# Gate and up products of an expert step in 512 columns instead of 256, with the weight split writing both chunks mixed

## The chip, the cores and the metric

The kernel runs on one core of one Trainium2 chip. The metric is the device time of one execution in microseconds (us), the median of several runs. TensorE is called PE here (its weight loads PEld), VectorE DVE, ScalarE ACT, GpSimd POOL, and SyncE, which issues the weight transfers, SP.

## The reference, cut to what matters

The program computes two model blocks over 256 tokens of width 1024. The last part of the second block is a mixture of eight experts, and it is the part that the change touches:

```python
N_EXPERTS = 8
TOP_K = 2
D_FF_EXPERT = 3584

def swiglu_2(x, w_gate, w_up, w_down):
    return (jax.nn.silu(x @ w_gate) * (x @ w_up)) @ w_down

def moe_swiglu(x, w_router, w_gate, w_up, w_down):
    ...
    for e in range(N_EXPERTS):
        y = y + combine[:, e:e + 1] * swiglu_2(xt, w_gate[e], w_up[e], w_down[e])
    return y.reshape(B, S, D)
```

All inputs are float32. Each expert has 3 x 1024 x 3584 weights, 44 MB.

## The kernel before, in words

The tokens that chose an expert are gathered by a product with a 0/1 matrix into `xe`, at most 128 of them, so that one pass of an expert is a product of 128 rows. A pass is made for each of the 8 experts (and more, if an expert has more than 128 tokens; in the profiled execution there are 8 passes). The first pass is written out, the others are a loop on the engines.

The hidden width of 3584 is walked in 14 steps of 256 (`MOE_PER`). The weights of a step are three chunks of 1 MB, 128 partitions x 2048 float32 each: a **gate** chunk (8 blocks of 128 rows x 256 columns, laid one behind the other), an **up** chunk of the same form, and a **down** chunk (2 blocks of 128 rows x 1024 columns). `MOE_ORDER` sets their order, which all engines follow: gate 0, up 0, gate 1, up 1, then gate s, up s, down s-2 for each step, and the last two downs at the end; 42 chunks in a pass.

A chunk goes through four engines:

- **SP** loads it into one of the 7 slots of `ring` (L510 to L515). It waits on `w_split`, the count of the chunks that are split, until the chunk 7 places before it has been split, and then issues the transfer.
- **ACT** copies it from the ring to `w_h`, rounded to the matmul type (`high_part`, L1237 to L1241). `w_h` and its partner `w_l` have 3 places (`SPLITS`), so the copy of chunk n+3 waits on `w_used`, which the first matmul of chunk n+1 raises. Between the copies ACT makes `silu` of the gate (L1452) and moves the transposed products out of PSUM (L1457).
- **DVE** takes the rest, `w_l` = ring - `w_h` (`low_part`, L1964 to L1968), and raises `w_split`. Between these it multiplies silu(gate) by up (L2064), and makes the rest of the transposed products (L2069).
- **PE** waits on `w_split` and multiplies with both parts. In `half_product` (L1043 to L1054) the stationary operand is a block of the tokens, `xe_h` or `xe_l` (128 x 128), and the moving operand is a block of 256 weight columns of `w_h` or `w_l`. Gate goes to columns 0 to 255 of PSUM bank s % 2, up to columns 256 to 511 of the same bank. For each of 8 row blocks k there are three products:

```python
o = 0 if part == "gate" else 256
out = psum[:, s % 2, o:o + 256]
for k in range(KD):
    first = nc.tensor.matmul(out, xe_h[:, k, :], wh[:, k, :], start=(k == 0), stop=False)
    ...
    nc.tensor.matmul(out, xe_h[:, k, :], wl[:, k, :], start=False, stop=False)
    last = nc.tensor.matmul(out, xe_l[:, k, :], wh[:, k, :], start=False, stop=(k == KD - 1))
```

That is 24 matmuls of 256 columns for a gate chunk and 24 for an up chunk. Both are done before `u_full` is raised, and only then does ACT take the silu. `expert_down` (L1064 to L1079) makes 12 matmuls of 512 columns for a down chunk, in turn into banks 4 and 5, and each matmul loads its own stationary operand. Two transposes (L1060) stand between a step's down and the next gate. A pass also has a gather (L1015), four pairs of matmuls that scatter the expert before it (L1031, L1032) and two more transposes.

Of the kernel before, what the change touches and what calls it, by code (L numbers as in the profile page):

```python
# [35 lines left out]
KD = D // P  # L36
SLOTS = 7
# [4 lines left out]
ALU = mybir.AluOpType  # L42
ACT = mybir.ActivationFunctionType
F32 = mybir.dt.float32
# [11 lines left out]
MOE_E = 8  # L56
MOE_PER = 3584 // 256
MOE_CHUNKS = 3 * MOE_PER
# [3 lines left out]
SPLITS = 3  # L62
# [44 lines left out]

MOE_ORDER = moe_order()
MOE_N = {c: n for n, c in enumerate(MOE_ORDER)}
LAST = MOE_PER - 1  # L110

SCATTER_AT = (3, 6)
# [112 lines left out]
CHUNKS = plan_chunks()  # L225
# [7 lines left out]
MOE_C0 = CHUNK_AT[("k8", "moe_gate", 0)]  # L233
# [4 lines left out]
def build(nc, a, out):  # L238
    with ExitStack() as ctx:
# [7 lines left out]
        ring = sb("ring", [P, SLOTS, CHUNK_F])  # L247
# [28 lines left out]
        psum = ctx.enter_context(nc.psum_tensor("psum", [P, BANKS, BF], F32))  # L276
# [34 lines left out]
        w_l = sb("w_l", [P, SPLITS, CHUNK_F], F32R)  # L311
# [74 lines left out]
        slot_full = [sem(f"slot_full{i}") for i in range(SLOTS)]  # L386
# [45 lines left out]
        w_high = sem("w_high")  # L432
        w_split = sem("w_split")
# [38 lines left out]
        def evacuated(eng, u):  # L472

            n = UNIT_AT[u]
            eng.wait_ge(bank_free[n % BANKS], n // BANKS + 1)

        def halves(ap):
            return ap.rearrange("p (b c) -> p b c", b=2)

# [3 lines left out]
        n = 0  # L483
# [14 lines left out]
        @block.sync  # L498
        def _(sp):

            sp.dma_start(h[:, :, :], a["x"].rearrange("a (b p) d -> p (a b) d", p=P)).then_inc(loads["x"], 16)
            for j in range(SLOTS):
                sp.dma_start(ring[:, j, :], a["stream"][j, :, :]).then_inc(slot_full[j], 16)
            with sp.Fori(1, MOE_C0 // SLOTS + 1) as r:
                for j in range(SLOTS):

                    sp.wait_ge(chunk_used, r * SLOTS - SLOTS + j + 1)
                    sp.dma_start(ring[:, j, :], a["stream"][bass.ds(r * SLOTS + j, 1), :, :]
                                 .rearrange("a p f -> (a p) f")).then_inc(slot_full[j], 16)
            with sp.Fori(MOE_C0 // SLOTS + 1, len(CHUNKS) // SLOTS) as r:  # L510
                for j in range(SLOTS):

                    sp.wait_ge(w_split, r * SLOTS + (j + 1 - SLOTS - MOE_C0))
                    sp.dma_start(ring[:, j, :], a["stream"][bass.ds(r * SLOTS + j, 1), :, :]
                                 .rearrange("a p f -> (a p) f")).then_inc(slot_full[j], 16)  # L515

            sp.wait_ge(table_ready, 1)
            n_over = sp.value_load(table[0:1, 1:2], min_val=0, max_val=OVER)
            with sp.If(n_over > 0):
                with sp.Fori(0, n_over) as p:  # L520
                    e = sp.value_load(table[0:1, bass.ds(p + 2, 1)], min_val=0, max_val=MOE_E - 1)
                    with sp.Fori(0, MOE_CHUNKS // SLOTS) as r:
                        for j in range(SLOTS):
                            sp.wait_ge(w_split, p * MOE_CHUNKS + r * SLOTS + (len(CHUNKS) - MOE_C0 - SLOTS + j + 1))
                            sp.dma_start(ring[:, j, :], a["stream"][bass.ds(e * MOE_CHUNKS + r * SLOTS + (MOE_C0 + j), 1), :, :]
                                         .rearrange("a p f -> (a p) f")).then_inc(slot_full[j], 16)

            for j in range(AHEAD):
                sp.wait_ge(w_split, n_over * MOE_CHUNKS + (len(CHUNKS) - MOE_C0 - SLOTS + j + 1))
                sp.dma_start(ring[:, j, :], a["stream"][MOE_C0 + j, :, :]).then_inc(slot_full[j], 16)  # L530


# [33 lines left out]
        def _(pe):  # L566
# [237 lines left out]
            for u in range(8):  # L804
                open_unit(pe, ("t_b", u))
                for j in range(4):
                    n = 4 * (u % 4) + j
                    last = nc.tensor.transpose(bank(("t_b", u))[:, j * P:(j + 1) * P],
                                               b_wide_f[u // 4][:, n * P:(n + 1) * P], ident[:, :])
# [5 lines left out]
            for u0 in range(0, BLK // 2, 4):  # L815
# [46 lines left out]
            for u in range(4):  # L862
                open_unit(pe, ("sgu", u))
                for j in range(2):
                    hd = 2 * u + j
                    for b in range(TB):
                        o = bank(("sgu", u))[:, j * TOK + b * P:j * TOK + (b + 1) * P]
# [169 lines left out]
            def split_pair(p, part, s, k):  # L1037

                n = MOE_N[(part, s)]
                pe.wait_ge(w_split, p * MOE_CHUNKS + (n + 1))  # L1040
                return [w[:, n % SPLITS, :].rearrange("p (k c) -> p k c", k=k) for w in (w_h, w_l)]

            def half_product(p, part, s):  # L1043
                wh, wl = split_pair(p, part, s, KD)
                o = 0 if part == "gate" else 256
                out = psum[:, s % 2, o:o + 256]
                for k in range(KD):
                    first = nc.tensor.matmul(out, xe_h[:, k, :], wh[:, k, :], start=(k == 0), stop=False)  # L1048
                    if k == 0:
                        first.then_inc(w_used, 1)  # L1050
                    nc.tensor.matmul(out, xe_h[:, k, :], wl[:, k, :], start=False, stop=False)  # L1051
                    last = nc.tensor.matmul(out, xe_l[:, k, :], wh[:, k, :], start=False, stop=(k == KD - 1))  # L1052
                if part == "up":
                    last.then_inc(u_full, 1)  # L1054

            def transpose_h(p, s):
# [24 lines left out]
            def one_expert(p, first):  # L1081

                pe.wait_ge(xe_split, p + 1)
                for s in range(MOE_PER):

                    pe.wait_ge(hT_ready, p * MOE_PER + (f0 + s - 1))
                    half_product(p, "gate", s)
                    half_product(p, "up", s)
                    if s in SCATTER_AT and not first:
                        b = SCATTER_AT.index(s)  # L1090
                        if b == 0:
                            pe.wait_ge(oe_split, p)
                            pe.wait_ge(pickT_ready, p)
                        else:

                            pe.wait_ge(y_added, p * 4 + 2)
                        scatter(p, b, (6, 7))
                    if s == GATHER_AT:

                        pe.wait_ge(pick_ready, p + 2)  # L1100
                        pe.wait_ge(y_added, p * 4 + 4)
                        gather(1)
                    if s == LAST:
                        transpose_h(p, s - 1)
                    if s >= 2:
                        if s == 2 and not first:

                            pe.wait_ge(oe_split, p)
                        expert_down(p, s - 2)
                    if 1 <= s < LAST:  # L1110
                        if s == PICK_AT + 1:

                            pe.wait_ge(pickT_ready, p + 1)
                        transpose_h(p, s - 1)
                    if s == PICK_AT:
                        transpose_pick()
                transpose_h(p, LAST)
                expert_down(p, LAST - 1)
                expert_down(p, LAST)
# [18 lines left out]
        def _(act):  # L1138
# [97 lines left out]

            def high_part(p, n):  # L1237

                act.wait_ge(slot_full[n % SLOTS], p * (16 * MOE_CHUNKS // SLOTS)
                            + 16 * (MOE_C0 // SLOTS + n // SLOTS + 1))  # L1240
                nc.scalar.activation(w_h[:, n % SPLITS, :], ring[:, n % SLOTS, :], ACT.Copy).then_inc(w_high, 1)  # L1241

            parts = [0]

# [63 lines left out]
            for u in range(8):  # L1308
                take_unit(act, ("t_b", u))
                n = 4 * (u % 4)  # L1310
# [186 lines left out]
        def _(dve):  # L1497
# [466 lines left out]
            def low_part(p, n):  # L1964

                dve.wait_ge(w_high, p * MOE_CHUNKS + (n + 1))
                V.tensor_tensor(w_l[:, n % SPLITS, :], ring[:, n % SLOTS, :], w_h[:, n % SPLITS, :].bitcast(F32),  # L1967
                                ALU.subtract).then_inc(w_split, 1)  # L1968


            V.tensor_copy(h_h[:, :, :], h[:, :, :]).then_inc(h_high, 1)
# [264 lines left out]
```

## Time and profile before

| | |
|---|---|
| median of 3 runs | 2394.29 us (2392.45 to 2394.78) |
| profiled execution, its own time | 2396.11 us |
| its span, first to last instruction | 2394.3 us |
| PE busy | 2210.5 us, 92% |
| PEld busy | 2043.9 us, 85% |
| DVE busy | 1563.7 us, 65% |
| ACT busy | 1190.5 us, 50% |
| mean granted clock of PE | 0.957 |
| HBM read | 539.05 MB |

The busy times are unions over the span, so that two overlapping instructions of an engine count once. The busy time of PE includes the modelled end of each matmul; what a matmul costs in a stream is read from the starts of two of them, not from its duration. The eight passes take the stretch from 1323 us to the end.

### The profile page before, as it was taken

How to read it: one execution, taken by the hardware profiler on the slowest of the kernel's cores; microseconds unless marked ns; L12 is line 12 of the kernel's file. 1: busy time of each engine (PE TensorE's matmuls, PEld its weight loads, DVE VectorE, ACT ScalarE, POOL GpSimd, SP SyncE). 2: the span in 40 equal slices, each digit the busy share in tenths (PEclk: the TensorE clock that was granted, in tenths of full speed). 3: DMA queues.
4: the chain of work that ended last, by engine and by line, in shares of the span. 5: the costliest groups of instructions: out<-in, count | busy, mean ns of one | idle time of the engine just before them, and what ended most of it. 6: DMA issues, size and time to landing. Idle time of an engine off the chain costs nothing.

```text
span 2394.3 us, 38794 instructions
## 1 busy us (share of the span) xinstructions
PE 2210.5 (92%) x15310; PEld 2043.9 (85%) x15310; DVE 1563.7 (65%) x1739; ACT 1190.5 (50%) x1206; POOL 9.8 (0%) x22
## 2 busy tenths in 40 slices
PE   7999987799889879989986999999999999999997
PEld 6888787799888779989876999989898998989896
DVE  6774144444555454454645789878787888888787
ACT  2300023334336533433642667767676766667674
POOL 0000000000000000000000000000000000000000
PEclk9999898899989989999997999999999999999998
DMA  7243241355543245554323799989898898989894
GB/s 285 105 152 112 71 157 71 115 184 191 196 176 124 99 137 188 187 199 177 115 97 123 275 358 337 355 310 348 307 351 320 341 339 326 357 311 356 309 348 154
DMA packets 76345, 542.45 MB, mean 227 GB/s; under 512 B 9121, under 2 KB 9265, under 8 KB 11810
## 3 DMA queue, kind: packets, MB, share of 16 engines
q1 hardware_dynamic: 72128, 524.32, 59.2%
q0 software_dynamic: 2080, 10.40, 1.2%
q10 hardware_dynamic: 1986, 5.41, 0.6%
q8 instruction: 132, 2.16, 0.4%
q14 instruction: 19, 0.16, 0.0%
HBM read 539.05 MB, written 1.05 MB: 226 GB/s over the span
## 4 chain that ended last, share of the span: by engine, by line
PE 86%; DVE 6%; ACT 4%; issue 3%; ACTq 0%; DVEq 0%
PE psum L750 11%; PE psum L1071 10%; PE psum L1048 9%; PE psum L1051 9%; PE psum L1052 9%; PE psum L595 6%; PE psum L656 6%; PE psum L642 6%; PE psum L762 5%; PE psum L608 3%; PE psum L621 2%; PE psum L1015 1%; DVE w_l L1967 1%; PE psum L1060 1%; PE psum L585 1%
## 5 line engine op out<-in xcount | busy, mean ns | idle before, releaser
L1967 DVE TENSOR_TENSOR w_l<-ring,w_h 128x2048 fp32r<-128x2048 f32 x338 | 773.7, 2291 | 177.6 <-ACT w_h L1241 176.5
L1241 ACT ACTIVATE w_h<-ring 128x2048 fp32r<-128x2048 f32 x338 | 647.0, 1914 | 166.4 <-PE psum L1048 122.4
L1048 PE MATMUL psum<-w_h,xe_h 128*128 128x256 f32 x1792 | 520.1, 290 | 23.0 <-issue 20.6
L1051 PE MATMUL psum<-w_l,xe_h 128*128 128x256 f32 x1792 | 511.5, 285 | 0.0
L1052 PE MATMUL psum<-w_h,xe_l 128*128 128x256 f32 x1792 | 511.4, 285 | 0.0
L1048 PEld LDWEIGHTS psum<-w_h,xe_h 128*128 128x128 f32 x1792 | 347.6, 194 | 26.0 <-issue 23.1
L1051 PEld LDWEIGHTS psum<-w_l,xe_h 128*128 128x128 f32 x1792 | 347.9, 194 | 0.0
L1052 PEld LDWEIGHTS psum<-w_h,xe_l 128*128 128x128 f32 x1792 | 347.5, 194 | 0.0
L1650 DVE TENSOR_TENSOR wf_l<-ring,wf_h 128x2048 fp32r<-128x2048 f32 x66 | 151.3, 2292 | 168.2 <-ACT wf_h L1235 168.2
L1624 DVE TENSOR_TENSOR wp_l<-ring,wp_h 128x2048 fp32r<-128x2048 f32 x54 | 123.7, 2292 | 168.5 <-ACT wp_h L1253 168.5
L750 PE MATMUL psum<-xf_h,wf_h 128*128 128x256 f32 x704 | 201.4, 286 | 4.5 <-DVE xf_l L1642 2.4
L750 PE MATMUL psum<-xf_l,wf_h 128*128 128x256 f32 x704 | 201.3, 286 | 0.0
L750 PE MATMUL psum<-xf_h,wf_l 128*128 128x256 f32 x704 | 201.2, 286 | 0.0
L1235 ACT ACTIVATE wf_h<-ring 128x2048 fp32r<-128x2048 f32 x66 | 125.9, 1910 | 125.4 <-PE psum L762 65.8
L1253 ACT ACTIVATE wp_h<-ring 128x2048 fp32r<-128x2048 f32 x54 | 103.0, 1910 | 157.5 <-PE psum L656 92.7
L750 PEld LDWEIGHTS psum<-xf_h,wf_h 128*128 128x128 f32 x704 | 137.1, 195 | 6.0 <-DVE xf_l L1642 2.8
L1071 PE MATMUL psum<-w_h,eT_h 128*128 128x512 f32 x448 | 141.2, 396 | 0.0
L1071 PE MATMUL psum<-w_h,eT_l 128*128 128x512 f32 x448 | 138.9, 391 | 0.0
L1071 PE MATMUL psum<-w_l,eT_h 128*128 128x512 f32 x448 | 138.8, 391 | 0.0
L750 PEld LDWEIGHTS psum<-xf_l,wf_h 128*128 128x128 f32 x704 | 137.0, 195 | 0.7
L750 PEld LDWEIGHTS psum<-xf_h,wf_l 128*128 128x128 f32 x704 | 137.0, 195 | 0.0
L656 PE MATMUL psum<-wp_h,xf_h 128*128 128x256 f32 x416 | 120.7, 290 | 16.0 <-DVE xf_l L1629 8.7
(340 smaller groups left out, 3720.7 us busy)
## 6 DMA issues: line engine op xcount, KB each, us to landing
ring<-in_stream SPq DMA_DIRECT2D x499, 1024.0 KB, 4.9
big<-in_bc POOLq DMA_DIRECT2D x11, 512.0 KB, 5.0
big<-in_na_bias POOLq DMA_DIRECT2D x2, 2048.0 KB, 8.0
big<-in_mem ACTq DMA_DIRECT2D x1, 1024.0 KB, 8.5
h<-in_x SPq DMA_DIRECT2D x1, 1024.0 KB, 7.5
r_k<-in_sgu_ln ACTq DMA_DIRECT2D x1, 1024.0 KB, 22.3
big<-in_s_c ACTq DMA_DIRECT2D x1, 1024.0 KB, 30.0
out_dram<-ysum ACTq DMA_DIRECT2D x1, 1024.0 KB, 4.0
```

The source lines that it names most:

```text
L595: last = nc.tensor.matmul(bank(unit)[:, j * TOK:(j + 1) * TOK], w[:, k, j * P:(j + 1) * P], act_T[:, k, :], start=(k == 0), stop=(k == KD ...
L642: last = nc.tensor.matmul(bank(unit)[:, j * TOK:(j + 1) * TOK], w[:, k, j * P:(j + 1) * P], x[:, k, :], start=(k == i == 0), stop=(k == KD ...
L656: last = nc.tensor.matmul(bank(unit)[:, b * 256:(b + 1) * 256], x[:, k, b * P:(b + 1) * P], w[:, k, :], start=(k == i == 0), stop=(k == KD ...
L750: last = nc.tensor.matmul(psum[:, b, j * TOK:(j + 1) * TOK], w[:, k, j * P:(j + 1) * P], x[:, k, :], start=(k == i == 0), stop=(k == KD - ...
L1048: first = nc.tensor.matmul(out, xe_h[:, k, :], wh[:, k, :], start=(k == 0), stop=False)
L1051: nc.tensor.matmul(out, xe_h[:, k, :], wl[:, k, :], start=False, stop=False)
L1052: last = nc.tensor.matmul(out, xe_l[:, k, :], wh[:, k, :], start=False, stop=(k == KD - 1))
L1071: last = nc.tensor.matmul(psum[:, 4 + c, :], x[:, s % 2, k, :], w[:, k, c * 512:(c + 1) * 512], start=(s == 0 and k == n == 0), stop=(s == ...
L1235: nc.scalar.activation(wf_h[:, n % SPLITS, :], ring[:, at % SLOTS, :], ACT.Copy).then_inc(wf_high, 1)
L1241: nc.scalar.activation(w_h[:, n % SPLITS, :], ring[:, n % SLOTS, :], ACT.Copy).then_inc(w_high, 1)
L1650: V.tensor_tensor(wf_l[:, n % SPLITS, :], ring[:, at % SLOTS, :], wf_h[:, n % SPLITS, :].bitcast(F32), ALU.subtract).then_inc(wf_split, 1)
L1967: V.tensor_tensor(w_l[:, n % SPLITS, :], ring[:, n % SLOTS, :], w_h[:, n % SPLITS, :].bitcast(F32), ALU.subtract).then_inc(w_split, 1)
```

## The change

The gate and up products of a step become one product of 512 columns, made in two halves over the rows. Each half takes 4 of the 8 row blocks k and makes three matmuls of 512 columns for each, 12 in all, which fill the whole PSUM bank: gate in its left 256 columns, up in the right ones.

For that, row block k of gate and row block k of up must lie side by side in `w_h` and `w_l`. The chunks in memory and the transfers are the same as before. The split does the mixing: the part called "gate" now takes blocks 0 to 3 of the gate chunk **and** blocks 0 to 3 of the up chunk, the part called "up" takes blocks 4 to 7 of both. It reads the two neighbouring slots of the ring (slots 6 and 0 with a negative step) in runs of 256 elements, and still handles 2048 elements a partition. So the copy of a "gate" part waits for the transfers of two chunks, and neither slot of the pair is free before the "up" part is split: `MOE_FREED` says so to SP, whose loop now runs over passes and names each chunk of a pass. The down chunks are split and used as before.

```diff
+MOE_FREED = [n + 2 if part == "gate" else n + 1 for n, (part, s) in enumerate(MOE_ORDER)]
...
+        def moe_parts(n, high, low):
+            part, s = MOE_ORDER[n % MOE_CHUNKS]
+            to = n % SPLITS
+            if part == "down":
+                return ring[:, n % SLOTS, :], high[:, to, :], low[:, to, :]
+            half = part == "up"
+            at = (n - half) % SLOTS
+            both = ring[:, at:at + 2, :] if at + 1 < SLOTS else ring[:, ::-at, :]
+            src = both[:, :, half * 1024:(half + 1) * 1024].rearrange("p a (k c) -> p a k c", k=4)
+            return (src,) + tuple(w[:, to, :].rearrange("p (k a c) -> p a k c", k=4, a=2) for w in (high, low))
...
-                    sp.wait_ge(w_split, r * SLOTS + (j + 1 - SLOTS - MOE_C0))
+                sp.wait_ge(w_split, p * MOE_CHUNKS + MOE_FREED[n])
...
-            def half_product(p, part, s):
-                wh, wl = split_pair(p, part, s, KD)
-                o = 0 if part == "gate" else 256
-                out = psum[:, s % 2, o:o + 256]
-                for k in range(KD):
-                    first = nc.tensor.matmul(out, xe_h[:, k, :], wh[:, k, :], start=(k == 0), stop=False)
...
+            def half_product(p, half, s):
+                wh, wl = split_pair(p, ("gate", "up")[half], s, 4)
+                out = psum[:, s % 2, :]
+                for i in range(4):
+                    k = 4 * half + i
+                    first = nc.tensor.matmul(out, xe_h[:, k, :], wh[:, i, :], start=(k == 0), stop=False)
...
+                    nc.tensor.matmul(out, xe_h[:, k, :], wl[:, i, :], start=False, stop=False)
+                    last = nc.tensor.matmul(out, xe_l[:, k, :], wh[:, i, :], start=False, stop=(k == KD - 1))
...
             def high_part(p, n):
...
-                act.wait_ge(slot_full[n % SLOTS], p * (16 * MOE_CHUNKS // SLOTS)
-                            + 16 * (MOE_C0 // SLOTS + n // SLOTS + 1))
-                nc.scalar.activation(w_h[:, n % SPLITS, :], ring[:, n % SLOTS, :], ACT.Copy).then_inc(w_high, 1)
+                gate = MOE_ORDER[n % MOE_CHUNKS][0] == "gate"
+                for c in ((n, n + 1) if gate else (n,)):
+                    act.wait_ge(slot_full[c % SLOTS], p * (16 * MOE_CHUNKS // SLOTS)
+                                + 16 * (MOE_C0 // SLOTS + c // SLOTS + 1))
+                src, high, _ = moe_parts(n, w_h, w_l)
+                nc.scalar.activation(high, src, ACT.Copy).then_inc(w_high, 1)
...
             def low_part(p, n):
...
-                V.tensor_tensor(w_l[:, n % SPLITS, :], ring[:, n % SLOTS, :], w_h[:, n % SPLITS, :].bitcast(F32),
-                                ALU.subtract).then_inc(w_split, 1)
+                src, high, low = moe_parts(n, w_h, w_l)
+                V.tensor_tensor(low, src, high.bitcast(F32), ALU.subtract).then_inc(w_split, 1)
```

PE, the seam between the first and the second half of step 0 of the first pass, before (L1048, L1051 and L1052 are the three products of a row block):

```order
L1048 MATMUL psum<-w_h,xe_h 128x256
L1051 MATMUL psum<-w_l,xe_h 128x256
L1052 MATMUL psum<-w_h,xe_l 128x256
L1048 MATMUL psum<-w_h,xe_h 128x256 [waits w_split]
L1051 MATMUL psum<-w_l,xe_h 128x256
L1052 MATMUL psum<-w_h,xe_l 128x256
```

and the same engine from the start of the first pass now, where the three products are L1070, L1073 and L1074:

```order
L1070 MATMUL psum<-w_h,xe_h 128x512 [waits w_split,hT_ready,xe_split]
L1073 MATMUL psum<-w_l,xe_h 128x512
L1074 MATMUL psum<-w_h,xe_l 128x512
L1070 MATMUL psum<-w_h,xe_h 128x512
L1073 MATMUL psum<-w_l,xe_h 128x512
L1074 MATMUL psum<-w_h,xe_l 128x512
```

The order of the three products is the same, each has twice the columns, and there are half as many: the 24 rows of a part became 12.

ACT, one step in the middle of a pass, before (L1241 is the copy to `w_h`, L1452 the silu, L1457 the move of the transposes):

```order
L1241 ACTIVATE w_h<-ring 128x2048 [waits slot_full5,w_used]
L1451 REGISTER_ALU
L1452 ACTIVATE e_silu<-psum 128x256 [waits up_full]
L1480 REGISTER_ALU
L1241 ACTIVATE w_h<-ring 128x2048 [waits slot_full6,w_used]
L1456 REGISTER_ALU
L1457 ACTIVATE eT_h<-psum 128x256 [waits hT_full]
L1480 REGISTER_ALU
L1239 REGISTER_ALU [waits w_used]
L1241 ACTIVATE w_h<-ring 128x2048 [waits slot_full0]
```

and the same step now (L1266, L1477, L1482):

```order
L1266 ACTIVATE w_h<-ring 128x2x4x256 [waits slot_full6,slot_full5,w_used]
L1476 REGISTER_ALU
L1477 ACTIVATE e_silu<-psum 128x256 [waits up_full]
L1505 REGISTER_ALU
L1266 ACTIVATE w_h<-ring 128x2x4x256 [waits slot_full6,w_used]
L1481 REGISTER_ALU
L1482 ACTIVATE eT_h<-psum 128x256 [waits hT_full]
L1505 REGISTER_ALU
L1263 REGISTER_ALU [waits w_used]
L1266 ACTIVATE w_h<-ring 128x2048 [waits slot_full0]
```

No instruction of ACT moved; the copies of gate and up have a pattern of 2 slots x 4 blocks x 256, and the gate copy waits for two slots.

## Rows read from the trace of the kernel before

**Rows 1.** Busy time by stretch; columns: PE, PEld, DVE, ACT, POOL, clock, DMA share, GB/s

```profile
10.00:20.00 10.00, 3.65 (x16) 3.28 (x16) 7.60 (x22) 4.88 (x11) 0.00 (x0) 1.00 1.03 418
1323.00:2394.30 1071.30, 1034.06 (x7280) 967.97 (x7280) 890.51 (x636) 727.10 (x587) 0.00 (x0) 0.98 0.86 324
...
1433.31:1561.12 127.81, 127.81 (x913) 119.77 (x912) 110.10 (x78) 90.56 (x73) 0.00 (x0) 1.00 0.93 346
1561.12:1694.25 133.13, 129.42 (x913) 121.26 (x912) 110.29 (x78) 90.64 (x73) 0.00 (x0) 0.99 0.88 332
...
1486.87:1495.58 8.71, 8.71 (x64) 8.17 (x63) 7.89 (x6) 6.41 (x5) 0.00 (x0) 1.00 0.98 357
```

**Rows 2.** Waits, 1340 to 2390 us: who waited for whom, us, times, longest

```profile
DVE w_l L1967 <- ACT w_h L1241: 168.2, 263, 4.1
ACT w_h L1241 <- PE psum L1048: 117.6, 115, 4.7
PE psum L1048 <- issue: 20.6, 6, 3.7
```

**Rows 3.** Groups by line: count, busy us, mean ns of one, idle before and its releaser

```profile
L1967 DVE TENSOR_TENSOR w_l<-ring,w_h 128x2048 fp32r<-128x2048 f32 x338 | 773.7, 2291 | 177.6 <-ACT w_h L1241 176.5
L1241 ACT ACTIVATE w_h<-ring 128x2048 fp32r<-128x2048 f32 x338 | 647.0, 1914 | 166.4 <-PE psum L1048 122.4
L1048 PE MATMUL psum<-w_h,xe_h 128*128 128x256 f32 x1792 | 520.1, 290 | 23.0 <-issue 20.6
L1071 PE MATMUL psum<-w_h,eT_h 128*128 128x512 f32 x448 | 141.2, 396 | 0.0
L1071 PEld LDWEIGHTS psum<-w_h,eT_h 128*128 128x128 f32 x448 | 78.2, 189 | 11.0
```

**Rows 4.** Order of time, PE, one step: start, us, engine, line

```profile
1486.72 0.63 PE L1071 MATMUL psum<-w_h,eT_h 128*128 128x512 f32 x2
...
1489.01 0.62 PE L1071 MATMUL psum<-w_h,eT_l 128*128 128x512 f32 x2
...
1490.28 0.28 PE L1052 MATMUL psum<-w_h,xe_l 128*128 128x256 f32 x1
...
1495.31 0.28 PE L1052 MATMUL psum<-w_h,xe_l 128*128 128x256 f32 x1
```

**Rows 5.** Order of time, one chunk from PE over ACT and DVE to PE

```profile
1495.43 0.63 PE L1071 MATMUL psum<-w_h,eT_h 128*128 128x512 f32 x2
...
1495.91 1.91 ACT L1241 ACTIVATE w_h<-ring 128x2048 fp32r<-128x2048 f32 x1
...
1497.85 2.29 DVE L1967 TENSOR_TENSOR w_l<-ring,w_h 128x2048 fp32r<-128x2048 f32 x1 [0.41 <-ACT w_h L1241]
...
1501.28 0.28 PE L1048 MATMUL psum<-w_h,xe_h 128*128 128x256 f32 x1
```

**Rows 6.** A slot of the ring: split, copy seven chunks later, landing, SP's wait

```profile
1480.40 2.29 DVE L1967 TENSOR_TENSOR w_l<-ring,w_h 128x2048 fp32r<-128x2048 f32 x1 [1.30 <-ACT w_h L1241]
...
1498.88 1.91 ACT L1241 ACTIVATE w_h<-ring 128x2048 fp32r<-128x2048 f32 x1
...
DMA to landing us min/median/max: 4.6/5.0/7.2
...
SPq L514 <- DVE w_l L1967: 810.5, 323, 6.0
```

**Rows 7.** Order of time, PE, behind the jump back of the loop of passes

```profile
1582.43 0.38 PE L1048 MATMUL psum<-w_h,xe_h 128*128 128x256 f32 x1 [3.71 <-issue]
...
1583.41 0.41 PE L1048 MATMUL psum<-w_h,xe_h 128*128 128x256 f32 x1
...
1585.97 0.42 PE L1048 MATMUL psum<-w_h,xe_h 128*128 128x256 f32 x1
```

**Rows 8.** Single lines: duration ns min/median/max, first and last start

```profile
L1551 DVE TENSOR_TENSOR h<-h,psum x8: 680/687/690, 345.0 to 449.3; 128x512 f32<-128x512 f32 x8
L1177 ACT ACTIVATE r_v<-psum x8: 580/588/597, 203.4 to 1100.0; 128x512 f32<-128x512 f32 x8
L1316 ACT ACTIVATE big<-psum x8: 1298/1394/1519, 76.7 to 85.0; 128x512 f32<-128x512 f32 x8
```

More of the change, by code:

```diff
@@ L509, in _, with load_moe @@
                                  .rearrange("a p f -> (a p) f")).then_inc(slot_full[j], 16)
-            with sp.Fori(MOE_C0 // SLOTS + 1, len(CHUNKS) // SLOTS) as r:
-                for j in range(SLOTS):
-                    sp.wait_ge(w_split, r * SLOTS + (j + 1 - SLOTS - MOE_C0))
-                    sp.dma_start(ring[:, j, :], a["stream"][bass.ds(r * SLOTS + j, 1), :, :]
-                                 .rearrange("a p f -> (a p) f")).then_inc(slot_full[j], 16)
+            def load_moe(p, n):
+                sp.wait_ge(w_split, p * MOE_CHUNKS + MOE_FREED[n])
+                j = n % SLOTS
+                sp.dma_start(ring[:, j, :], a["stream"][bass.ds(p * MOE_CHUNKS + (MOE_C0 + n + SLOTS), 1), :, :]
+                             .rearrange("a p f -> (a p) f")).then_inc(slot_full[j], 16)
+            with sp.Fori(0, MOE_E - 1) as p:
+                for n in range(MOE_CHUNKS):
+                    load_moe(p, n)
+            for n in range(MOE_CHUNKS - SLOTS):
+                load_moe(MOE_E - 1, n)
             sp.wait_ge(table_ready, 1)
@@ L521, in _ @@
                     e = sp.value_load(table[0:1, bass.ds(p + 2, 1)], min_val=0, max_val=MOE_E - 1)
[L522 to L526, printed above, removed]
+                    for n in range(MOE_CHUNKS):
+                        before_n = n - SLOTS
+                        sp.wait_ge(w_split, p * MOE_CHUNKS + ((MOE_E - 1) * MOE_CHUNKS + MOE_FREED[before_n] +
+                                                              (0 if before_n < 0 else MOE_CHUNKS)))
+                        sp.dma_start(ring[:, n % SLOTS, :], a["stream"][bass.ds(e * MOE_CHUNKS + (MOE_C0 + n), 1), :, :]
+                                     .rearrange("a p f -> (a p) f")).then_inc(slot_full[n % SLOTS], 16)
             for j in range(AHEAD):
-                sp.wait_ge(w_split, n_over * MOE_CHUNKS + (len(CHUNKS) - MOE_C0 - SLOTS + j + 1))
+                sp.wait_ge(w_split, n_over * MOE_CHUNKS + ((MOE_E - 1) * MOE_CHUNKS + MOE_FREED[MOE_CHUNKS - SLOTS + j]))
                 sp.dma_start(ring[:, j, :], a["stream"][MOE_C0 + j, :, :]).then_inc(slot_full[j], 16)
@@ L1041, in split_pair @@
                 return [w[:, n % SPLITS, :].rearrange("p (k c) -> p k c", k=k) for w in (w_h, w_l)]
-            def half_product(p, part, s):
-                wh, wl = split_pair(p, part, s, KD)
-                o = 0 if part == "gate" else 256
-                out = psum[:, s % 2, o:o + 256]
-                for k in range(KD):
-                    first = nc.tensor.matmul(out, xe_h[:, k, :], wh[:, k, :], start=(k == 0), stop=False)
-                    if k == 0:
+            def half_product(p, half, s):
[4 more added lines that the diff above has]
+                    first = nc.tensor.matmul(out, xe_h[:, k, :], wh[:, i, :], start=(k == 0), stop=False)
+                    if i == 0:
                         first.then_inc(w_used, 1)
-                    nc.tensor.matmul(out, xe_h[:, k, :], wl[:, k, :], start=False, stop=False)
-                    last = nc.tensor.matmul(out, xe_l[:, k, :], wh[:, k, :], start=False, stop=(k == KD - 1))
-                if part == "up":
+                    nc.tensor.matmul(out, xe_h[:, k, :], wl[:, i, :], start=False, stop=False)
+                    last = nc.tensor.matmul(out, xe_l[:, k, :], wh[:, i, :], start=False, stop=(k == KD - 1))
+                if half == 1:
                     last.then_inc(u_full, 1)
@@ L1086, in one_expert @@
                     pe.wait_ge(hT_ready, p * MOE_PER + (f0 + s - 1))
-                    half_product(p, "gate", s)
-                    half_product(p, "up", s)
+                    half_product(p, 0, s)
+                    half_product(p, 1, s)
                     if s in SCATTER_AT and not first:
```

## The prediction

> **What bounds the kernel now.** I began with the busy times by stretch, to see which engine is full in the passes of the experts, the only part that changes. PE is busy for 1034 of 1071 us there; in the first whole pass for 127.81 of 127.81 us, and in a single step for all of its 8.71 us, while DVE is busy for 7.89 us and ACT for 6.41 us of the same step [rows 1]. The list of waits says the same from the other side: DVE waits for ACT, ACT waits for PE's first matmul of a chunk, and PE waits for nobody but the instruction stream, 6 times for 20.6 us [rows 2]. That is the jump back of the loop of passes, 3.71 us in the row that I show [rows 7]. So in the steps the pace is PE's, and ACT and DVE are led by it. The groups by line give the rest: 1792 matmuls for each of the three gate and up products, 5376 of 256 columns in all, and a weight load for each matmul of the down products too (448 loads for 448 matmuls in the group shown) [rows 3].
>
> The duration of a matmul (290 ns for 256 columns, 396 ns for 512 [rows 3]) is no price, since they overlap. The price is the distance between starts. In one step, 42 matmuls of 256 columns begin between 1490.28 and 1495.31 us, which is 119.8 ns each; 10 of 512 columns begin between 1486.72 and 1489.01 us, 229.0 ns each [rows 4].
>
> **The change, part by part.**
>
> *PE.* 5376 matmuls of 256 columns go, 2688 of 512 columns come, and their weight loads are halved with them. A pair of the old ones took 2 x 119.8 = 239.6 ns, a new one at the pace of the down products takes 229.0 ns: 10.6 ns less, 2688 times, 28.5 us. In a step this is 24 x 10.6 ns = 0.25 us, from 8.71 to 8.46 us. Since PE is full, all of it lies on the path.
> From this goes what runs at the low clock. Behind the jump back the matmuls of 256 columns are 213.3 ns apart (1583.41 to 1585.97 us, 12 of them [rows 7]), which is the 1.2 GHz level and exactly the time of their columns; there a pair gives back nothing. With some 3.4 us of it at no more than 7 jumps, 16 old matmuls each, that is at most 56 pairs, 0.6 us. I take 0.4 us off and keep 28.1 us.
> The bounds of the new distance: at the full clock the columns alone need half of 2 x 213.3, 213.3 ns, so no matmul of 512 columns can be closer; that would be 26.3 ns a pair and 70.7 us. The other end is that the 13 ns above the columns (119.8 - 106.7) are paid per column, 239.6 ns, no gain. The nearest row is the down product, which has the same columns, the same type and its own weight load. It differs in one thing: it goes in turn to two banks, the new product stays in one. The old one stayed in one too, and its excess (13 ns) is no larger than that of the down product (16 ns), so the bank seems to cost nothing. I take 229.0.
>
> [...]
>
> *ACT and DVE.* Nothing is added or moved: 338 copies of 1914 ns and 338 subtractions of 2291 ns [rows 3], still of 2048 elements, but two of three now read runs of 256 from two slots and write runs of 256. The nearest rows of such runs: the residual add on DVE, two runs of 256 at a distance of 1024, takes 687 ns for 512 elements, and ACT's write into two such runs 588 ns [rows 8], which per element is no more than what the long contiguous ones pay. I cost them at nothing. A bound above is the ACT copy that writes single elements far apart, 1394 ns for 512 [rows 8], 2.4 times as much. Below nothing I see no reason to go.
> What hides them is their lead over PE. The chunk that I followed: the down product's first matmul at 1495.43 us lets ACT start at 1495.91, DVE ends the split at 1497.85 + 2.29 = 1500.14, and PE needs it at 1501.28 [rows 5]: 1.14 us in hand after a way of 4.71 us. The new product in between is 0.13 us shorter for this chunk, and for the down chunk, which has gate and up in its window, 0.25 us. So the lead shrinks to about 0.9 us and holds. DVE's share of a step goes from 7.89 of 8.71 to 7.89 of 8.46 us.
>
> *SP and the transfers.* The gate copy needs the up chunk, one place early, and the gate slot is freed one place late. In the rows: a slot is free at 1480.40 + 2.29 = 1482.69 us, its next content is copied at 1498.88 us, and a landing takes 5.0 us, so 11.2 us are in hand [rows 6]. In a step the up chunk goes into the slot that a gate chunk leaves, which meets both losses, two places of 8.46 / 3 = 2.8 us: 5.6 us remain. The second transfer of a pair that is freed together lands up to 2.9 us later, but it is a down chunk, which loses nothing else. SP has been waiting for splits for 810 us of these 1050 [rows 6]. I cost it at nothing; if this cover went, ACT's gate copy would be late first, then DVE and PE.
>
> **The sum.** 2396.1 us of the profiled execution's own time (its span is 2394.3) less 28.1 is 2368.0. The median of the runs lies 1.8 us below that execution, so 2366.2; I forecast **2366 us**. About 0.2% (4.8 us) is what a measurement of this kernel tells from no change. With the new distance 4 ns off on either side the gain is 39 or 17 us, 2355 to 2377.
>
> **The rivals.**
>
> 1. *The transfers set the pace of a step.* A step moves 3.146 MB. DMA moved 357 GB/s at a share of 0.98 in the step shown [rows 1]; if 1.00 is the limit, that is 364 GB/s and 8.64 us a step, and only 0.07 of the 0.25 us is won: 112 x 0.07 = 8 us, **2386**. For it: that share. Against: 418 GB/s at a share of 1.03 early in the kernel [rows 1], SP's long waits, a pass as a whole needs only 332 to 346 GB/s, and 5.6 us in hand against 12 steps x 0.18 = 2.2 us that a pass could fall behind before its end gives it back. Chance 0.05.
> 2. *The excess is paid per column in one bank.* The distance is 240 ns, and nothing changes: **2394**. For it: the down product's excess is larger than that of 256 columns, and it has two banks. Against: it would have to be 11 ns larger still. This is also the case in which the change does not do what it says. Chance 0.05.
> 3. *The mixed split is slow, and DVE or ACT becomes the bound.* This ends on the other side. DVE has 7.89 us of work in a step; if each of its two mixed subtractions costs over 0.41 us (18%) more, 7.89 + 2 x 0.41 = 8.71 us, the step is longer than before; from 0.29 us on it eats the gain. ACT would do it later: the way of 4.71 us and one product of 2.75 us make 7.46 us, so an extra of 1.25 us in a copy breaks even. At the price of the scattered copy, 2.37 times [rows 8], a copy takes 2.62 us more and ACT needs 6.41 + 2 x 2.62 = 11.65 us a step, 2.9 us more than now, 112 times: 2394 + 325, **about 2720**. For it: no row has a pattern of 2 x 4 x 256 over two slots. Against: runs of 256 cost nothing where the trace has them. Chance 0.06 for slower, 0.05 for a part of the gain eaten, around 2380.
> 4. *The weight load was what held the 256 columns back, and 512 get near their columns.* Distance below 0.225 us, **2325 to 2355**. For it: halving the loads leaves twice the time for each. Against: the down products have the same and stand at 229.0. Chance 0.03.
>
> **How the numbers follow.** The forecast has 0.76. Faster by over 0.2% takes it, rivals 1 and 4 and most of the eaten gain: 0.87. Slower is 0.06, within 0.2% 0.07. The range begins at 2355, the 4 ns, and reaches to 2387 to take in the transfers and the eaten gain; outside are no change, slower, and the large gain, about 0.14, with a little for a distance off by more.
>
> **What would show it.** Right: in the changed profile 896 matmuls of 512 columns on each of the three lines (2688), 229 ns apart; a step of 8.46 us; the mixed copies still 1.91 us and the subtractions 2.29 us; PE waiting for nobody in the steps; the same jump of 3 to 4 us. Wrong: waits of PE for `w_l` (the split), waits of ACT for the ring's transfers (rival 1), a distance near 240 or 215 ns (rivals 2 and 4), or subtractions of over 2.7 us (rival 3).

## The result, and the profile after

The changed kernel takes **2334.98 us** (median of 4 runs, 2331.11 to 2337.16) beside 2393.37 us for the kernel before (4 runs, 2391.61 to 2394.78): a ratio of 0.9754, 95% interval 0.9740 to 0.9769. That is 58 us less where 28 were forecast, and below the range. The profiled execution took 2336.91 us, with a span of 2335.1 us, 59.2 us less than before.

The groups by line of the page after, with the row of the instruction queue (packets, MB, share), which answer to [rows 3]:

```profile
PE 2169.7 (93%) x12622; PEld 1893.5 (81%) x12622; DVE 1560.2 (67%) x1739; ACT 1190.9 (51%) x1206; POOL 9.8 (0%) x22
...
q8 instruction: 73, 1.20, 0.2%
...
L1993 DVE TENSOR_TENSOR w_l<-ring,w_h 128x2048 fp32r<-128x2048 f32 x338 | 773.5, 2291 | 120.4 <-ACT w_h L1266 113.8
L1266 ACT ACTIVATE w_h<-ring 128x2048 fp32r<-128x2048 f32 x338 | 647.6, 1916 | 141.1 <-PE psum L1070 97.4
L1070 PE MATMUL psum<-w_h,xe_h 128*128 128x512 f32 x896 | 360.6, 402 | 2.4 <-DVE xe_l L2074 2.4
```

There are 896 matmuls of 512 columns on a line. The mixed copies take 1916 ns (1914 before) and the subtractions 2291 ns as before: the mixed split costs nothing, as forecast. Two things are new. The row of L1070 has no `issue` behind it any more, where L1048 had 20.6 us; and the instruction queue has 73 packets, where the page before says

```profile
q8 instruction: 132, 2.16, 0.4%
```

Busy time by stretch after (columns as in [rows 1]): the whole part of the experts, one step, the first whole pass, and the first one that holds a jump back of the loop.

```profile
1323.00:2335.10 1012.10, 995.48 (x4592) 819.65 (x4592) 888.03 (x637) 727.14 (x587) 0.00 (x0) 0.99 0.86 342
...
1484.43:1492.85 8.42, 8.42 (x42) 6.93 (x40) 7.69 (x6) 6.31 (x5) 0.00 (x0) 1.00 0.91 337
...
1426.17:1550.09 123.92, 123.92 (x575) 102.15 (x574) 109.92 (x79) 90.51 (x73) 0.00 (x0) 1.00 0.90 356
1550.09:1674.16 124.07, 124.07 (x575) 102.16 (x574) 109.91 (x79) 90.61 (x73) 0.00 (x0) 1.00 0.90 355
```

A step went from 8.71 to 8.42 us. The first pass went from 127.81 to 123.92 us. The next one went from 133.13 to 124.07 us [rows 1], and only here is the surprise: before, a pass with a jump was 5.3 us longer than the one without, now it is 0.15 us longer, and the five after it are as long as the first (123.92 to 123.96 us). The order of time on PE at that jump (the last down product, then the next step's first matmuls, the answer to [rows 7]) shows no gap:

```profile
1570.40 0.61 PE L1093 MATMUL psum<-w_h,eT_l 128*128 128x512 f32 x2
1570.96 0.50 PE L1070 MATMUL psum<-w_h,xe_h 128*128 128x512 f32 x1
1571.30 0.40 PE L1073 MATMUL psum<-w_l,xe_h 128*128 128x512 f32 x1
```

The jump has a row of its own: the branch at the end of TensorE's loop, by source line (duration ns min/median/max, first and last start), in the kernel before

```profile
L1127 PEldq COMPARE_BRANCH  x7: 83/6240/6594, 1575.5 to 2371.3; - x7
```

and after:

```profile
L1149 PEldq COMPARE_BRANCH  x7: 76/208/247, 1567.9 to 2311.6; - x7
```

The shortest of the seven is the one that leaves the loop. The six that jump back last 5.98 to 6.59 us before and 0.21 to 0.25 us after. The sequencer comes to the first branch about 3 us before the matmuls in front of it are through (1575.5 us, and the last down product starts at 1578.3), so that of its 6.6 us only 3.71 show as idle time of PE.

And the waits between 1340 and 2330 us, the answer to [rows 2] (who waited for whom, us, times, longest): PE's weight loads wait for the split 14 times, 3.8 us together (once, 0.3 us, before), its matmuls never, and neither waits for instructions any longer; ACT still waits for PE, not for transfers.

```profile
DVE w_l L1993 <- ACT w_h L1266: 105.4, 178, 3.7
ACT w_h L1266 <- PE psum L1070: 92.9, 110, 1.2
ACT w_h L1266 <- PE psum L1093: 43.6, 30, 3.4
PEld psum L1070 <- DVE w_l L1993: 3.8, 14, 0.4
```

**Where the 59.2 us are.** From gather to gather of PE (L1015 before, L1036 after): the work up to the second gather is 3.6 us shorter (116.17 to 112.53), the first whole pass 3.9 (127.81 to 123.93), the six with a jump 52.0 (795.7 to 743.8 together), the end 0.3 longer. Taken at the first whole pass's 3.9, the pitch gave 3.6 + 3.9 + 6 x 3.9 = 31 us. The other 28.6 us are the jumps: 20.6 us of stalls, and 8.0 us that are left. Nearly all of these belong to stretches at half the clock (0.50 from 1583.00 to 1586.40 us), 3.4 us long, behind five of the six stalls: 16 matmuls that each take 213.3 instead of 119.8 ns, five times, are 7.5 us.

So the question for the experiments was why the jump back got free. **Theory A**: the halved number of instructions. In the traces TensorE has 1899 records a looped pass before and 1227 after (matmuls, weight loads, and 79 register, semaphore and branch instructions); so short a body can be held, and the jump needs no fetch. **Theory B**: something else that the change touched at the turn of a pass (SyncE's loop has 42 loads a round where it had seven; the mixed split's timing). **Theory C**: the width, for the clock part. Instruction DMA between 1600 and 2300 us speaks for A; before it goes on,

```profile
q8 instruction: 47, 0.77, 0.4%
```

and after, no row of q8 stands in that stretch.

### The profile page after: what moved, and what is told of

Its sections match the earlier page's. It is cut to its first block, busy times and chain, and to the rows that moved or that the text cites. A ratio compares the mean times of both kernels' runs of the same rounds, so it can differ in the third digit from the quotient of the medians.

```text
span 2335.1 us, 33178 instructions
## 1 busy us (share of the span) xinstructions
PE 2169.7 (93%) x12622; PEld 1893.5 (81%) x12622; DVE 1560.2 (67%) x1739; ACT 1190.9 (51%) x1206; POOL 9.8 (0%) x22
## 4 chain that ended last, share of the span: by engine, by line
PE 89%; DVE 5%; ACT 4%; issue 2%; ACTq 0%; DVEq 0%
PE psum L1093 13%; PE psum L771 11%; PE psum L1070 9%; PE psum L1074 9%; PE psum L1073 9%; PE psum L616 7%; PE psum L677 6%; PE psum L663 6%; PE psum L783 5%; PE psum L629 3%; PE psum L642 2%; PE psum L1036 2%; PE psum L1082 1%; PE psum L606 1%; ACT wp_h L1278 1%
## 5 line engine op out<-in xcount | busy, mean ns | idle before, releaser
L1993 DVE TENSOR_TENSOR w_l<-ring,w_h 128x2048 fp32r<-128x2048 f32 x338 | 773.5, 2291 | 120.4 <-ACT w_h L1266 113.8
L1266 ACT ACTIVATE w_h<-ring 128x2048 fp32r<-128x2048 f32 x338 | 647.6, 1916 | 141.1 <-PE psum L1070 97.4
L1070 PE MATMUL psum<-w_h,xe_h 128*128 128x512 f32 x896 | 360.6, 402 | 2.4 <-DVE xe_l L2074 2.4
L1074 PE MATMUL psum<-w_h,xe_l 128*128 128x512 f32 x896 | 350.9, 392 | 0.0
L1073 PE MATMUL psum<-w_l,xe_h 128*128 128x512 f32 x896 | 350.1, 391 | 0.0
L1070 PEld LDWEIGHTS psum<-w_h,xe_h 128*128 128x128 f32 x896 | 168.8, 188 | 38.2 <-DVE w_l L1993 3.8
L1074 PEld LDWEIGHTS psum<-w_h,xe_l 128*128 128x128 f32 x896 | 168.6, 188 | 36.8
L1073 PEld LDWEIGHTS psum<-w_l,xe_h 128*128 128x128 f32 x896 | 169.1, 189 | 32.4
```

Of the source, the lines that this page charges most:

```text
L1070: first = nc.tensor.matmul(out, xe_h[:, k, :], wh[:, i, :], start=(k == 0), stop=False)
L1073: nc.tensor.matmul(out, xe_h[:, k, :], wl[:, i, :], start=False, stop=False)
L1074: last = nc.tensor.matmul(out, xe_l[:, k, :], wh[:, i, :], start=False, stop=(k == KD - 1))
L1266: nc.scalar.activation(high, src, ACT.Copy).then_inc(w_high, 1)
L1993: V.tensor_tensor(low, src, high.bitcast(F32), ALU.subtract).then_inc(w_split, 1)
```

## The experiments

Medians come with the kernel before run on the same chip beside them: 2396.53 us (2390.71 to 2398.81, 13 runs) for the first four, 2396.42 us (one run) for the last four, which have one run each themselves.

### e1: the old width in the new kernel

```diff
-                for i in range(4):
-                    k = 4 * half + i
-                    first = nc.tensor.matmul(out, xe_h[:, k, :], wh[:, i, :], start=(k == 0), stop=False)
...
+                cols = ((0, 512),) if False else ((0, 256), (256, 512))
+                for lo, hi in cols:
+                    for i in range(4):
+                        k = 4 * half + i
+                        o, wi = out[:, lo:hi], (wh[:, i, lo:hi], wl[:, i, lo:hi])
+                        first = nc.tensor.matmul(o, xe_h[:, k, :], wi[0], start=(k == 0), stop=False,
+                                                 skip_group_check=True)
...
```

Two sums of a bank are interleaved here, which changes those sums (the result is off by a relative 0.025); every instruction is executed.

> The changed kernel, with each product of 512 columns made as two of 256 again; the mixed split, its buffers and SyncE's new loop stay. TensorE's loop body has about 1900 instructions again, as before the change, in place of about 1230. Theory A (the jump back of TensorE's expert loop cost 3 to 4 us and a half-clock stretch behind it because the body was too long to stay at hand; the shorter body ended that): the pitch is 120 ns a product of 256 columns, the six waits called issue (20.6 us) and the five stretches of half clock are back, instruction DMA goes on through the loop (some 47 packets between 1600 and 2300 us), and the time is that of the kernel before, 2390 to 2396 us. Theory B (the stall went because of SyncE's new loop or of the mixed split's timing): the pitch is 120 ns, but no stall and no low clock, so 2393 - 20.6 - 8 = about 2364 us. Theory C (the width of the product itself keeps the clock up): the stall stays away, the low clock comes back: 2373 us.

Measured: 2392.2 us (10 runs), ratio 0.9979, interval 0.9967 to 0.9991: the time of the kernel before, less 0.1 to 0.3%, with a span of 2394.9 us. All came back together: the stalls (waits, 1340 to 2330 us), the low clock behind five of the six (0.66 over the 5 us behind each), and instruction DMA (1600 to 2300 us).

```profile
PE psum L1073 <- issue: 19.7, 6, 3.5
```

```profile
q8 instruction: 47, 0.77, 0.4%
```

The mixed split and SyncE's new loop are both in this kernel. They neither take the stall away nor cost time. B falls.

### e2: the jump taken out of the kernel before

```diff
-            with pe.Fori(1, n_pass) as p:
+            for p in range(1, MOE_E):
                 one_expert(p, False)
+            with pe.If(n_pass > MOE_E):
+                with pe.Fori(MOE_E, n_pass) as p:
+                    one_expert(p, False)
```

> The kernel before, with 256-column products and its old split, where TensorE's passes 1 to 7 are written out one behind the other, and the loop stands only for passes beyond the eighth, which do not occur here. No jump back is taken. Theory A: each looped pass of 133.1 us loses the 3.5 us of the jump's stall and the half-clock stretch behind it and comes to the first pass's 127.8; with 20.6 us of stalls and about 8 us of low clock gone, 2393 - 28.6 = about 2365 us. Instruction DMA still runs through all passes, since each is new code. Theory B (the stall belongs to something else at the turn of a pass, such as SyncE's loop of seven loads or the copies there): the stalls stay at the turns, 2390 to 2396 us. Theory D (fetching code at all, not the jump, is what stalls): also 2390 to 2396 us or more, with the waits spread through the passes.

Measured: **2367.11 us**, ratio 0.9885, interval 0.9867 to 0.9904. All seven passes take 127.92 or 127.93 us. In the waits the matmuls have none called issue, and the weight loads hardly anything:

```profile
PEld psum L1048 <- issue: 2.4, 7, 0.3
```

though fresh code is fetched all the time (1600 to 2300 us):

```profile
q8 instruction: 40, 0.66, 0.4%
```

Fetching in a straight line costs next to nothing (a pass is 0.12 us longer than the 127.81 us of the first one before); the jump does cost. That is the answer to theory D. The row also gives the size of a packet in instructions: 700 us are 5.47 passes, which have 1851 records each in this kernel (no loop, so fewer register instructions), for 40 packets of 16 KB, so about 253 a packet. The loop before, 1899 records, is thus some 7.5 packets long, the one after, 1227, 4.8. A block is in what follows the code that one packet brings. The starts of the packets in e5 give 255 instructions for each (below); with that figure the loops are, by estimate, 7.4 and 4.8 blocks.

### e3: the new kernel's code spread out

```diff
                 for s in range(MOE_PER):
+                    if not first and s >= 1:
+                        pe.addr_align(256, max_nops=0)
```

> The changed kernel with its 512-column products, where each step of a looped pass begins at a fresh 16 KB block of TensorE's code; the same instructions run, with about one branch more a step (13 a pass), but the loop's code lies over some 14 blocks in place of 5. Theory A (the body's extent in code decides): pitch 227 ns as in the changed kernel, but the stall of 3 to 4 us at each jump back and the half clock behind it are back, 2335 + 20.6 + 8 = about 2363 us, and up to 13 x 6 short waits more if a branch to the next block costs anything (0.1 us each would be 8 us). Instruction DMA goes on through the loop. Theories B and C (split, SyncE's loop or width): nothing changes, 2333 to 2338 us.

Measured: **2360.4 us** (2359.96 to 2362.6), ratio 0.9859, interval 0.984 to 0.9877. Products are 512 wide and the instructions are those of the changed kernel, but the loop lies over more blocks, and the stall is back, with 82 packets between 1600 and 2300 us. The six jumps back last 5.68 to 6.33 us. The order of time on PE at its first jump:

```profile
1570.26 0.61 PE L1093 MATMUL psum<-w_h,eT_l 128*128 128x512 f32 x2
1574.20 0.49 PE L1070 MATMUL psum<-w_h,xe_h 128*128 128x512 f32 x1 [3.33 <-issue]
```

The first whole pass, without a jump but with 12 of the 13 short branches of a round, takes 123.97 us beside 123.93: these cost nothing. Against the forecast of 2363 us 2.6 us are missing; here only three of the six stalls were followed by the low clock (last section). So neither the width (C) nor the number of executed instructions decides, but how much code the loop lies over.

### e4: a hint in the kernel before

```diff
-            with pe.Fori(1, n_pass) as p:
+            with nc.Fori(1, n_pass, engines=bass.OrderedEngineSet([pe.engine]), hint_back_edge=True) as p:
```

The kernel before with `hint_back_edge=True` on TensorE's loop, called the hint; nothing else differs.

> [...] Theory A: the jump finds its target fetched, the six stalls of 20.6 us and the low clock behind them go, 2393 - 28.6 = about 2365 us, while instruction DMA still goes on through the loop (the body is as long as it was). If the hint takes away only a part of the stall, it lies between 2365 and 2393. Theory B: no change, 2390 to 2396 us.

Measured: **2365.46 us** (2364.4 to 2368.59), ratio 0.9876, interval 0.9858 to 0.9894. In the trace the hint is one instruction more at the head of each looped pass, BRANCH_PREFETCH_HINT at L1127, 7 times, 31 to 55 ns. That it lets the jump find its target fetched was my assumption; e8 tests it. Busy time by stretch, the first whole pass and the next:

```profile
1430.32:1558.12 127.80, 127.80 (x912) 119.75 (x911) 110.08 (x79) 90.57 (x73) 0.00 (x0) 1.00 0.92 346
1558.12:1685.93 127.81, 127.81 (x912) 119.76 (x911) 110.08 (x79) 90.61 (x73) 0.00 (x0) 1.00 0.92 345
```

All passes are now the first one's length, and the six jumps back last 0.22 to 0.26 us. One thing I expected wrongly: instruction DMA does not go on. The page has 77 packets, and between 1600 and 2300 us there is none. So a loop of 7.4 blocks can be held, and without the hint something takes its head away. The next three runs ask what.

### e5, e6, e7: how long a loop is held

e5 is the kernel before with the loop's head at the start of a block. e6 and e7 are the changed kernel with the same head, and with pairs of 256 columns (as in e1) from step 10 or step 7 on:

```diff
-            with pe.Fori(1, n_pass) as p:
+            with nc.Fori(1, n_pass, engines=bass.OrderedEngineSet([pe.engine]), head_slot={pe.engine: 0}) as p:
...
+                cols = ((0, 512),) if s < 10 else ((0, 256), (256, 512))
```

> The kernel before (256-column products, no hint), where the first instruction of TensorE's loop is put at the start of a 16 KB block of code, so that its 1900 instructions (7.4 blocks) lie in 8 blocks and not in 9. Theory A1 (eight blocks are held, and it is only the loop's ninth that is too much): no stall, no instruction DMA after the first round, about 2365 us. Theory A2 (the sequencer fetches one or two blocks ahead, past the loop's end, and these take the place of its head; the hint of the run before stopped that): the stalls and the nine or ten packets a pass stay, 2390 to 2396 us.

> The changed kernel, with products of 512 columns in steps 0 to 9 of 14 and pairs of 256 in the last four, the loop's head at a block's start: about 1420 instructions, 5.6 blocks, so 6. The pitch gain is 10/14 of 31 us. Theory A2 with one or two blocks fetched ahead: 6 and 2 are no more than 8, so no stall and no instruction DMA after the first round: 2335 + 9 = about 2344 us. If the stall comes with anything over the changed kernel's 5 blocks: 2344 + 28 = 2372 us. In this kernel two sums of a bank are interleaved in its last four steps, which changes those sums; every instruction is still executed.

> The same with 512 columns in steps 0 to 6 and pairs of 256 in the other seven: about 1566 instructions, 6.1 blocks, so 7. Half of the pitch gain: 2335 + 15.5 = 2351 us without the stall, 2378 us with it. Theory A1 (eight held, none lost to fetching ahead): no stall. Theory A2 with one block ahead: no stall; with two blocks ahead (7 and 2 are over 8): stalls, and about seven to nine packets a pass. In this kernel two sums of a bank are interleaved in its last seven steps, which changes those sums; every instruction is still executed.

Measured: e5 2399.77 us, e6 2345.77 us, e7 2352.86 us, one run each; what follows rests on the rows of their traces and not on a few us of these times. The waits of e5 between 1600 and 2300 us, and its instruction packets there:

```profile
PE psum L1048 <- issue: 16.9, 5, 3.6
```

```profile
q8 instruction: 48, 0.79, 0.4%
```

e6 has no packet of q8 in that stretch and e7 one; neither has a wait called issue, and e7's looped passes after the first take 125.90 us, each of them. The jumps back last 6.09 to 6.46 us in e5, 0.21 to 0.24 us in e6 and e7. So a loop in 6 or 7 blocks jumps back for nothing, and one in 8 pays 3.4 us (16.9 us in 5). (e5 is 3 us slower than the kernel before beside it: going into the loop costs 0.9 us of idle time there, and all six of its stalls were followed by the low clock.) The count of packets tells why. In e5 the loop lies in 8 blocks, but 48 packets in 700 us, at 132.8 us a pass, are 9.1 a pass: one more than the loop has. That is theory A2 with one block: the block behind the loop's end is fetched ahead, nine blocks then go in turn through room for eight, and each is gone when it is wanted. With 7 and 1 nothing is refetched (e7), nor with the hinted loop of 7.4 blocks, which needs room for eight at the least (e4). The kernel before, 47 packets at 132.6 us a pass, has 8.9, which fits 8 and 1; e3's 82 at 128.0 us are 15.0, its 14 and 1.

The times of the packets bear this out. In e5 the packets of a round start at 1582.0 us (inside the stall), 1587.9, 1601.3, 1618.9, 1634.4, 1652.8, 1670.4, 1688.0 and 1702.3 us, and the next round's first at 1714.7, inside the next stall. From the third on each comes as TensorE enters a block: when the ninth starts, 1785 of the round's 1899 instructions have begun, which is 255 for each of seven blocks, beside the 253 a packet of e2. The loop ends in its eighth block, so the ninth packet is code behind its end. The kernel before has the same nine in a round, the ninth 13.6 us ahead of the head's (1566.1 and 1579.7 us); e4 has no packet after 1553.1 us, so the hint stopped the one behind the end as well. No trace here names the address that a packet came from, so this stays inferred, from counts and times.

### e8: the hint on a loop too long to hold

The diff is those of e3 and e4 together, on the changed kernel.

> The changed kernel with its code spread over some 14 blocks (as e3), and the hint at the loop's head (as e4). This loop is too long to be held in any case. If the hint has the target of the jump fetched in time, the six stalls and low-clock stretches go although 15 packets a pass go on: about 2335 to 2338 us. If the hint of e4 helped only because it kept blocks beyond the loop's end from taking the place of its head, it does nothing here: 2360 us.

Measured: 2334.49 us (one run). Passes take 123.97 to 124.10 us, no wait is called issue, the jumps back last 0.36 to 0.37 us, and the packets go on (1600 to 2300 us):

```profile
q8 instruction: 79, 1.29, 0.7%
```

The hint has the target fetched in time; it does not depend on the loop fitting. The packets show it: 79 at 124.0 us a pass are 14.0 and not the 15 that I expected, so the odd one is gone, and the last one ahead of the second jump starts at 1677.9 us, 12.2 us before the branch (1690.1 us). In e3 one starts at 1683.4 us, and then the head's at 1698.7, behind its branch (1695.1 us). With e3's short branches all still there, they are not the cause of e3's stall either.

**The four corners.**

| | jump stalls | jump does not stall |
|---|---|---|
| products of 256 | 2396.5 (before), 2392.2 (e1) | 2367.1 (e2), 2365.5 (e4) |
| products of 512 | 2360.4 (e3) | 2335.0 (after), 2334.5 (e8) |

(The changed kernel's runs stood beside a kernel before of 2393.4 us, 3 us below that of the others.) Down a column the width gives 30 to 36 us; along a row the jump gives 25 to 31 us. Within these few us the two effects add up, and no kernel tried beats the changed one by more than a measurement can tell.

## Why the prediction was wrong

**What bounds the kernel: right.** PE's pitch set the steps, and it does so after: PE is busy for all of 8.42 us of a step and all of 123.92 us of a pass.

**The new distance: right mechanism, somewhat small.** I took 229.0 ns from the down products. In a product's run the new ones start closer. In order of time, 12 of them from the first to the last of these rows, 2.72 us, are 226.7 ns each:

```profile
1487.03 0.39 PE L1074 MATMUL psum<-w_h,xe_l 128*128 128x512 f32 x1
...
1489.75 0.39 PE L1074 MATMUL psum<-w_h,xe_l 128*128 128x512 f32 x1
```

The first of a product takes longer, so that a whole pass gives 3.88 us for 336 pairs, 11.5 ns a pair, where I said 10.6. The down products do the same: of my ten, the last six (1487.65 to 1489.01 us) are 226.7 ns apart too, and only the slower start of the run makes 229.0. So two banks cost nothing against one. The term measured 31 us instead of 28.5, well inside my bound of 4 ns. That a pair gives back nothing at the low clock holds too: at a clock of 0.50 the 256 columns take 213.3 ns (1.2 columns a ns), and in e3, behind the second jump, 8 matmuls of 512 columns start from 1702.40 to 1705.39 us, 427 ns apart, twice that. That at the full clock no distance can be shorter than half of this, 213.3 ns, was my estimate; what a product's run shows is 226.7 ns.

**The mixed copies, the ring, SP: right, nothing.** The copies and subtractions kept their times, and e1, which has all of this with the old pitch, lies 0.1 to 0.3% below the kernel before, not above it. The lead over PE shrank, and at 14 places to nothing for a weight load (3.8 us in all, at most 0.4 us each), but no matmul came later for it. The rivals 1, 2 and 3 fall: DMA moves 356 GB/s at a share of 0.90 in a pass and PE does not wait for it, the distance is not 240 ns, and no mixed copy is slower. Rival 4's range, 2325 to 2355, holds the measured time, but not by its mechanism: the distance is 226.7 ns, not below 225, and half of the gain is elsewhere.

**The step that failed: "the same jump of 3 to 4 us".** I had the row of the stall [rows 7] and its sum, 20.6 us [rows 2], and left it in place after the change, without a reason, as if it were a constant of the loop. My paragraph on the low clock likewise took 0.4 us off the gain for the stretches behind the jump, as if they would stay. Both hang on the jump's miss, and the change removed it by halving the matmuls and weight loads of gate and up: the looped body went from 1899 to 1227 records, from 8 blocks to 5 or 6, and its jumps back from 6 us to 0.2. e1 puts the number back and gets the stall back; e3 keeps the number, spreads the code and gets it back too; e2 and e4 take the miss from the kernel before and gain 29 and 31 us. The missing term was 20.6 + 8.0 = 28.6 us; taken from 2366 it gives 2337, 2 us above the measured median. The 2.5 us of the distance would account for that, but the runs of the changed kernel alone spread over 6 us, so that the last 2 us prove nothing.

What could have been read ahead of time: the row of q8 on the page before, 132 packets, of which 47 lie in the loop's rounds between 1600 and 2300 us, and the row of the branch, 6.2 us. A loop whose code still arrives in its later rounds is not held, and a change that removes a third of its instructions can change that. How many blocks are held, no row of before tells; the runs do: loops in 5 to 7 blocks fetch next to nothing in their later rounds (after, e6 and e7: none, none and one packet in 700 us), one in 8 blocks fetches 9.1 packets a round (e5). At e5's 255 instructions a block, 1899 instructions are 7.4 blocks and 1227 are 4.8.

## What to carry to other kernels

Count the instructions of a hot loop on its fullest engine, and look whether instruction packets go on in its later rounds: if they do and the branch at its end lasts microseconds, or a gap called issue stands at each jump back, the stall and the half clock behind it are a price that a shorter body, a written-out loop or one hint removes, here 25 to 31 us for six jumps. And when an edit removes instructions by the hundred, no stall of the sequencer may be carried over into the forecast as a constant.

## What was not expected of the hardware

- TensorE's loop of 6.1 blocks of code (e7) jumps back for nothing, one of 7.4 blocks (e5, head at a block's start) pays 3.4 us on average at each jump. By the counts above, room for eight blocks holds a loop of seven (e7, one packet in 700 us), and one of eight only with the hint (e4, no packet; e5, 48).
- A jump back that misses takes the sequencer some 6 us (5.7 to 6.6 us in before, e1, e3 and e5), of which 2.84 to 3.71 us show as idle time of PE; one that hits takes 0.2 to 0.4 us, and none of it shows.
- A stall of this size has a second price, but not always. Busy time by stretch, 5 us behind the first and the fifth of the six jumps of the kernel before:

```profile
1582.43:1587.43 5.00, 5.00 (x29) 5.00 (x30) 2.56 (x2) 3.04 (x3) 0.00 (x0) 0.66 0.60 246
2113.63:2118.63 5.00, 5.00 (x41) 5.00 (x42) 2.55 (x2) 4.50 (x3) 0.00 (x0) 1.00 0.71 290
```

The first has a granted clock of 0.66 over its 5 us, that is 3.4 us at half the clock (0.50 from 1583.00 to 1586.40 us), and 29 matmuls; the fifth has a clock of 1.00 and 41. The stall's length doesn't decide it: in the order of time 3.71 us ahead of the first, 3.25 us ahead of the fifth, but 3.15 us ahead of the third, which was followed by the low level too. Five of six were followed by the low level before. In e5 all six were; in e3 it was every other one. There, 5 us behind its second to sixth jump the clock was

```profile
1701.36:1706.36 5.00, 5.00 (x15) 3.97 (x16) 2.39 (x2) 2.96 (x3) 0.00 (x0) 0.66 0.94 357
1830.08:1835.08 5.00, 5.00 (x22) 4.16 (x23) 2.38 (x2) 4.33 (x3) 0.00 (x0) 1.00 0.91 356
1957.57:1962.57 5.00, 5.00 (x15) 4.00 (x16) 2.39 (x2) 2.95 (x3) 0.00 (x0) 0.66 0.91 378
2086.42:2091.42 5.00, 5.00 (x22) 4.17 (x23) 2.39 (x2) 4.33 (x3) 0.00 (x0) 1.00 0.90 364
2213.51:2218.51 5.00, 5.00 (x15) 3.98 (x16) 2.39 (x2) 2.96 (x3) 0.00 (x0) 0.66 0.93 356
```

What decides between the two is open; no run was made for it.
